# Gate products of a recurrence as 64-row passes, and a new order of ScalarE's work around them, in a hybrid transformer block

## The reference, cut to what matters

```
xb = xf.reshape(B, S, 16, 64)
r   = sigmoid(einsum('bsni,nij->bsnj', xb, w_a) + b_a)
i_g = sigmoid(einsum('bsni,nij->bsnj', xb, w_x) + b_x)
log_a = -8 * r * softplus(-lam)
a = exp(log_a)
mult = sqrt(-expm1(2 * log_a))          # 1 at the first token
h_t = a_t * h_(t-1) + mult * i_g * xf   # along the tokens
y_rnn = h * gelu(g_rnn)
```

## Time and profile before

| | |
|---|---|
| median of 3 runs | 2143.26 us (2142.67 to 2144.76) |
| the profiled execution | 2143.2 us, of it 2141.4 us span (first to last instruction) |
| TensorE busy | 2124.1 us, 99% of the span |
| TensorE weight loads | 2093.2 us, 98% |
| VectorE busy | 1684.1 us, 79% |
| ScalarE busy | 1023.3 us, 48% |
| GpSimd busy | 342.5 us, 16% |

### The profile page before, as it was taken

The page is one execution under the profiler, slowest core; times in us unless marked ns, Lnnn a source line. Parts: engine busy times, 40 slices in busy tenths (PEclk is TensorE's granted clock), DMA queues, the critical chain, the costliest instruction groups (busy, mean ns, idle before and its releaser), DMA issues.

```text
span 2141.4 us, 44252 instructions
## 1 busy us (share of the span) xinstructions
PE 2124.1 (99%) x18238; PEld 2093.2 (98%) x18238; DVE 1684.1 (79%) x2297; ACT 1023.3 (48%) x1287; POOL 342.5 (16%) x428
## 2 busy tenths in 40 slices
PE   9999999999999999999999999999999999999998
PEld 8999999999999999999999999999999999999997
DVE  7777777778855877888888888888887867767876
ACT  6555554456322554444444444444444545445543
POOL 0222222222100001212112121121211001012002
PEclk9999999999999999999999999999999999999999
DMA  5788988888543435887887878788888658679645
GB/s 178 163 195 208 209 190 204 200 186 193 155 130 99 153 112 171 233 217 212 220 217 220 225 208 221 214 224 222 230 219 277 193 155 290 177 190 278 204 138 187
DMA packets 238754, 423.84 MB, mean 198 GB/s; under 512 B 17008, under 2 KB 151792, under 8 KB 237312
## 3 DMA queue, kind: packets, MB, share of 16 engines
q1 hardware_dynamic: 147776, 256.84, 36.2%
q0 software_dynamic: 88224, 159.97, 36.0%
q10 hardware_dynamic: 2592, 4.72, 0.6%
HBM read 382.64 MB, written 89.16 MB: 220 GB/s over the span
## 4 chain that ended last, share of the span: by engine, by line
PE 93%; DVE 3%; issue 1%; ACT 1%; DMA 1%; POOL 1%; POOLq 0%; DVEq 0%; ACTq 0%
PE bank L2086 29%; PE bank L2088 29%; PE bank L2087 29%; PE bank L2470 2%; PE bank L2165 1%; PE bank L2178 1%; DVE w_all L1226 1%; DMA act_lo_f<-t_spill 1%; PE bank L2190 0%; PE bank L2189 0%; ACT act_hi L1144 0%; ACT w_all L775 0%; PE bank L2250 0%; DMA t_spill<-h_out 0%; DVE tsum L1804 0%
## 5 line engine op out<-in xcount | busy, mean ns | idle before, releaser
L2086 PE MATMUL bank<-act_hi,w_all 128*128 128x256 f32 x3272 | 909.9, 278 | 5.2 <-DVE w_all L1226 2.5
L2088 PE MATMUL bank<-act_hi,w_all 128*128 128x256 f32 x3272 | 903.9, 276 | 0.0
L2087 PE MATMUL bank<-act_lo,w_all 128*128 128x256 f32 x3272 | 903.8, 276 | 0.0
L2086 PEld LDWEIGHTS bank<-act_hi,w_all 128*128 128x128 f32 x3272 | 614.2, 188 | 11.4 <-issue 4.0
L2087 PEld LDWEIGHTS bank<-act_lo,w_all 128*128 128x128 f32 x3272 | 614.3, 188 | 0.7 <-issue 0.2
L2088 PEld LDWEIGHTS bank<-act_hi,w_all 128*128 128x128 f32 x3272 | 614.3, 188 | 0.0
L2086 PE MATMUL bank<-tsum,w_all 128*128 128x256 f32 x1280 | 353.5, 276 | 0.0
L2088 PE MATMUL bank<-tsum,w_all 128*128 128x256 f32 x1280 | 353.3, 276 | 0.0
L2087 PE MATMUL bank<-tsum,w_all 128*128 128x256 f32 x1280 | 353.3, 276 | 0.0
L1138 ACT ACTIVATE w_all<-raw_s 128x1024 fp32r<-128x1024 f32 x172 | 182.9, 1063 | 242.8 <-PE bank L2088 222.1
L1226 DVE TENSOR_TENSOR w_all<-raw,w_all 128x1024 fp32r<-128x1024 f32 x134 | 164.1, 1225 | 133.6 <-ACT w_all L775 131.9
(11 more groups left out here) (401 smaller groups left out, 3524.2 us busy)
## 6 DMA issues: line engine op xcount, KB each, us to landing
raw<-weights SPq DMA_DIRECT2D x262, 512.0 KB, 4.2
w_sums<-weights POOLq DMA_DIRECT2D x96, 512.0 KB, 6.9
raw_s<-weights SPq DMA_DIRECT2D x84, 512.0 KB, 5.4
raw_s<-weights POOLq DMA_DIRECT2D x84, 512.0 KB, 5.7
raw_a<-weights SPq DMA_DIRECT2D x66, 512.0 KB, 5.6
raw_s<-w_sums SPq DMA_DIRECT2D x48, 512.0 KB, 5.2
t_spill<-h_out POOLq DMA_DIRECT2D x48, 256.0 KB, 3.7
act_lo_f<-t_spill POOLq DMA_DIRECT2D x11, 1024.0 KB, 10.0
```

Of the source, the lines that this page charges most:

```text
L2086: pe.matmul(dst, ah, bh, start=start, stop=False, skip_group_check=goes_on)
L2087: pe.matmul(dst, ah, bl, start=False, stop=False, skip_group_check=goes_on)
L2088: return pe.matmul(dst, al, bh, start=False, stop=stop, skip_group_check=goes_on)
```

## The change

**TensorE.** The gate products become six passes of 64 rows. Pass (t, e) multiplies the 64 rows of head e with both gates' 64x64 blocks side by side, 128 columns of weights, into bank e. The passes of the two heads alternate. The block-diagonal zeros are no longer computed. Bank 0 holds gate a of head 0 over gate x of head 0; bank 1 holds gate x of head 1 over gate a of head 1.

**ScalarE.** There are four sigmoids of 64 partitions in place of two of 128. Tanh and exponential are separate now. The exponential moves behind the softmax's `exps(p * 2, 0, 4)` (in the opening behind the root). In the first pair the tanh moves ahead of the keys' high part. In the loop the split of unit u+6 moves from behind the sigmoids to ahead of the squares.

**GpSimd and VectorE.** `gw` is 128 x 2 x 64, loaded by three transfers in place of one, each time. `decay` waits for one count more, since the exponential now comes last of the three functions.

```diff
-            pool.dma_start(gw[:], gate_w[0]).then_inc(gw_landed, 16)
+            def load_gates(p):
+                pool.dma_start(gw[0:HD], gate_w[p, 0:HD, :, 0:HD]).then_inc(gw_landed, 16)
+                for g in range(2):
+                    pool.dma_start(gw[HD:P, 1 - g], gate_w[p, HD:P, g, HD:P]).then_inc(gw_landed, 16)
+            load_gates(0)
...
             def gates(p, a, b):
-                act.wait_ge(gates_done, p)
-                act.activation(rg[:], a[:], ACT.Sigmoid, bias=col("b_a", p - 1)).then_inc(gates_taken, 1)
-                act.activation(ig[:], b[:], ACT.Sigmoid, bias=col("b_x", p - 1)).then_inc(gates_taken, 1)
+                act.wait_ge(gates_done, p * 2)
+                h0, h1 = slice(0, HD), slice(HD, P)
+                for dst, bias, parts in ((rg, "b_a", ((h0, a, h0), (h1, b, h1))), (ig, "b_x", ((h0, a, h1), (h1, b, h0)))):
+                    for h, bank, at in parts:
+                        act.activation(dst[h], bank[at], ACT.Sigmoid, bias=col(bias, p - 1)[h]).then_inc(gates_taken, 1)
...
-                if first:
-                    split(u + 6, 0, MORE_MIX)
+                split(u + 6, 0, MORE_MIX)
                 attention_square(p)
                 recurrent_square(p)
-                if first:
-                    gates(p + 1, PT[0], PT[1])
-                else:
-                    gates(p + 1, PT[0], PT[1])
-                    split(u + 6, 0, MORE_MIX)
-                    gate_exponentials(p + 1)
+                gates(p + 1, PT[0], PT[1])
+                gate_tanh(p + 1)
                 high_of(k_hi, ev, k_taken, p, k_hi_done)
                 split(u + 7, 1, MORE_MIX)
-                if first:
-                    gate_exponentials(p + 1)
                 gate_root(p + 1)
                 exps(p * 2, 0, 4)
+                gate_exp(p + 1)
...
             def decay(p):
-                dve.wait_ge(gate_funcs, p * 3 - 1)
+                dve.wait_ge(gate_funcs, p * 3)
...
-                for g, bank in enumerate((a, b)):
-                    last = product(bank[:], (gw_hi[:, g], gw_lo[:, g]), (xc_hi[:], xc_lo[:]), True, True)
-                last.then_inc(gates_done, 1)
+                for t, (w, x) in enumerate(((gw_hi, xc_hi), (gw_hi, xc_lo), (gw_lo, xc_hi))):
+                    for e, bank in enumerate((a, b)):
+                        h = slice(HD * e, HD * e + HD)
+                        last = pe.matmul(bank[:], w[h].rearrange("p a n -> p (a n)"), x[h], start=t == 0, stop=t == 2)
+                        if t == 2:
+                            last.then_inc(gates_done, 1)
```

More of the change, by code:

```diff
@@ L244, in block_kernel @@
         pick = sb_in(mix, "pick", [2, P])
-        gw = sb_in(mix, "gw", [2, P])
-        gw_hi = sb_in(mix, "gw_hi", [2, P], F32R)
-        gw_lo = sb_in(mix, "gw_lo", [2, P], F32R)
+        gw = sb_in(mix, "gw", [2, HD])
+        gw_hi = sb_in(mix, "gw_hi", [2, HD], F32R)
+        gw_lo = sb_in(mix, "gw_lo", [2, HD], F32R)
+        sb_in(mix, "rest_of_gw", [6 * HD])
         stats = sb_in(mix, "stats", [3, QT])
@@ L642, in _ @@
                 pool.wait_ge(gw_split, p)
-                pool.dma_start(gw[:], gate_w[p]).then_inc(gw_landed, 16)
+                load_gates(p)
                 pool.wait_ge(s_taken, p * 6)
@@ L802, in gates, with gate_tanh, gate_root, gate_exp @@
             def gates(p, a, b):
-                act.wait_ge(gates_done, p)
-                act.activation(rg[:], a[:], ACT.Sigmoid, bias=col("b_a", p - 1)).then_inc(gates_taken, 1)
-                act.activation(ig[:], b[:], ACT.Sigmoid, bias=col("b_x", p - 1)).then_inc(gates_taken, 1)
-            def gate_exponentials(p):
-                act.wait_ge(gates_taken, p * 2)
+                act.wait_ge(gates_done, p * 2)
[3 more added lines that the diff above has]
+                        act.activation(dst[h], bank[at], ACT.Sigmoid, bias=col(bias, p - 1)[h]).then_inc(gates_taken, 1)
+            def gate_tanh(p):
+                act.wait_ge(gates_taken, p * 4)
                 act.activation(tt[:], rg[:], ACT.Tanh, scale=one_col(lam4, p - 1)).then_inc(gate_funcs, 1)
+            def gate_root(p):
+                act.wait_ge(gate_funcs, p * 3 - 2)
+                act.activation(st[:], tt[:], ACT.Sqrt).then_inc(gate_funcs, 1)
+            def gate_exp(p):
                 act.activation(ae[:], rg[:], ACT.Exp, scale=one_col(lam8, p - 1)).then_inc(gate_funcs, 1)
-            def gate_root(p):
-                act.wait_ge(gate_funcs, p * 3 - 1)
-                act.activation(st[:], tt[:], ACT.Sqrt).then_inc(gate_funcs, 1)
             def gelu(p):
@@ L822, in gate_weights @@
             def gate_weights(p):
-                act.wait_ge(gw_landed, p * 16 + 16)
+                act.wait_ge(gw_landed, p * 48 + 48)
                 act.activation(gw_hi[:], gw[:], ACT.Copy).then_inc(gw_hi_done, 1)
@@ L965, in _ @@
             act.wait_ge(negc_stored, 16)
-            gate_exponentials(1)
+            gate_tanh(1)
             gate_root(1)
+            gate_exp(1)
             pair(1, True)
@@ L2212, in pair_scores @@
                 pe.wait_ge(k_split, p + 1)
-                pe.wait_ge(gates_taken, p * 2 + 2)
+                pe.wait_ge(gates_taken, p * 4 + 4)
                 scores((0, 1))
@@ L2308, in _ @@
             pe.wait_ge(negc_ready, 1)
-            pe.wait_ge(gates_taken, 2)
+            pe.wait_ge(gates_taken, 4)
             for e, bank in enumerate((PT[0], PT[2])):
```

## The result

The changed kernel takes **2148.78 us** (median of 11 runs, 2147.53 to 2150.49), against 2143.83 us for the kernel before beside it. The ratio is 1.0024, 95% interval [1.0016, 1.0032]: slower by a quarter of a per cent. (One of the eleven executions of the kernel before took 8002.83 us; the ratio leaves it out, and the median of the other ten is 2143.70.) The forecast was 2145.2, its range ended at 2147.8; the time lies outside. The sign of the sum was right, its size was not: +5.1 us against the kernel beside it, +5.5 against the 2143.26 on which the forecast stood, where +2.0 was forecast. The profiled execution took 2148.92 us, its span is 2146.9.

The account below looks back on a forecast made before the run. TensorE was taken to bound the kernel, working through practically the whole span. Terms +1.2 - 0.3 + 1.4 + 1.5 - 1.8 = +2.0 us on 2143.26 gave 2145.2 us, 8-in-10 range 2141.2 to 2147.8.

Parts of the forecast that it names:

- The passes: Gate passes on TensorE: two 64-row passes run side by side, 1.08 us in place of 1.40, saving 0.32 us per pair.
- The opening: Kernel start: three gate loads ahead of the constants delay the warming passes and first real pass, +1.2 us; high end +1.8 more.
- The exponential ahead of the first pair: ScalarE before the first pair: exponential behind root and a second table load makes the weight split and transposes late, +1.4 us.
- The first pair: First pair's gates: four sigmoids and the tanh ahead of the keys' high part make the scores late, +1.5 us.
- The loop: Six loop pairs: load and exponential taken out pay for the added sigmoids, so 0.30 us each is saved, -1.8 us.
- if the loop's scores wait: Sign to look for in the loop: no wait at the scores expected; a wait there would show the sum wrong.
- keys' low part ends late in all six pairs: Loop rival: sigmoids at 0.69 and a split wait 0.5 later lose 0.7 us per pair, 2149.8 us; chance 0.11.
- The sum: Whole kernel: opening +1.2, its gates -0.3, exponential +1.4, first pair +1.5, loop -1.8, together +2.0 us, 2145.2 us.

Follow-up runs that it names:

- the mended kernel with 12 warming matmuls: The changed kernel with one packed gate load behind the opening's constants, exponential and tanh moved back, a one-column sigmoid loading the table early, 12 warming matmuls: 2141.46 us.

## Why the prediction was wrong, point by point

- **The passes** (0.32 us a pair, side by side): right. 0.3 measured, and 0.33 a pair where nothing else is late.
- **The opening** (+1.2): +2.3 in the trace. The loads were sized rightly (+1.13 at the first warming pass). The term mis-sized is the pace of the warming records: the working took it to quicken after as long a time as before, and its high end had all of them slow, +1.8 on top of the loads. +1.15 on top came. In other executions it was less; it belongs in the range as noise of some 0.7 us between executions of one opening. By the first scores 0.5 of it was won back, where 0.3 was reckoned.
- **The exponential ahead of the first pair** (+1.4): right, 1.3 between the first scores and the transposes. Only the place differs: TensorE waits 1.4 at a weight unit 3.6 us ahead of the transposes, and 0.6 there.
- **The first pair** (+1.5): +1.85. The order of instructions was right. From the squares to the keys' high part it is 5.94 us where 5.49 was reckoned, since all four sigmoids are 0.71 apart in place of 0.58; the squares came 0.14 earlier than reckoned and took some of that back.
- **The loop** (-1.8): +1.0 up to the last pair's scores. This step failed, and with it the sum: it makes 2.8 us of the difference, the opening with its gates 0.9, the first pair 0.35. The working had the split and the squares right to within 0.03 us, counted from the first unit pass behind the gates, and then took "a 64-row sigmoid at the same 0.58 as a 128-row one". From the first sigmoid to the tanh 2.42 us was reckoned and 2.95 came. 0.39 of these 0.53 us are the three distances of 0.71. The other 0.14 are the tanh's wait for the last sigmoid, taken at 0.1: the tanh starts 0.82 behind it, in the run with two 128-row sigmoids too. The working also left "0.2 us to spare" between the end of the keys' low part and the scores, where 0.24 passes between the two in the loop in any case. So there was no spare, and the 0.53 became scores that start 0.52 late (the list of waits books 0.46). With the passes' 0.3 won, each pair lost 0.17. The prediction had named the sign: if the loop's scores wait, the sum is wrong there.
- The working counted the loop's gain as one of the passes. The trace with the passes alone shows that they gain nothing there unless the split moves. That link was not seen; that the change moved the split as well is luck for this term.
- **The rival** "keys' low part ends late in all six pairs" was the right mechanism, with a chance of 0.11. Its condition, sigmoids at 0.69, came; its second one, a split 0.5 late, did not, and was not needed. It was given 0.7 us a pair for the two together, and 2149.8 in all. The argument against it (no load between sigmoid and tanh) said nothing on the distance of sigmoids.
- **The sum.** Forecast: 0.9, 1.4, 1.5, -1.8. Measured in the trace: 1.8, 1.3, 1.85, +1.0, and -0.4 further on in the kernel, where nothing was changed (not followed up).

## What to carry to other kernels

When a change splits an instruction by rows, look in the trace for two neighbours whose rows change as the new ones will; the distance of starts is the price, not the length that each shows. A saving on the bound engine is only as good as the spare time of the next chain: with 0.2 us left, count the time from the end of the last write to the start of the reader too, and a reader's wait for its semaphore. And before a gain is booked, look for short gaps (0.1 to 0.3 us) that no list of waits shows at the places the engine will now reach earlier.

## What the runs showed of the hardware that was not expected

- **ScalarE: change of rows.** 512-column sigmoids start 0.57 to 0.59 us apart when the second reads and writes the rows of the first, or some of them; 0.68 to 0.71 when it reads other rows, 0.70 to 0.71 when it writes other rows. The Trainium skill, ScalarE: Activation LUTs, "What ACT_TABLE_LOAD costs", has back-to-back activations overlap by about 93 ns. The traces agree for neighbours with the same rows (0.68 long, 0.59 apart) and not for the others, where the overlap is gone (0.69 long, 0.71 apart).
- **VectorE beside GpSimd's DMA issues.** Four softmax scalings per half pair take 1.27 us together in most places and up to 2.3 in some. In the run with the passes alone, first pair, VectorE and GpSimd:

```profile
153.28 2.29 DVE L1347 TENSOR_SCALAR sm<-sm,stats 128x512 f32<-128x512 f32 x4
...
153.04 1.47 POOL L631 DMA_DIRECT2D w_sums<-weights  x1 [5.68 <-DMA w_sums<-weights]
153.82 2.14 POOL L632 DMA_DIRECT2D w_sums<-weights  x1
```

  and in the kernel before, at the same place:

```profile
153.25 1.28 DVE L1346 TENSOR_SCALAR sm<-sm,stats 128x512 f32<-128x512 f32 x4
...
153.94 1.53 POOL L630 DMA_DIRECT2D w_sums<-weights  x1 [6.72 <-DMA w_sums<-weights]
```

  GpSimd began 0.9 us earlier and worked beside all four. VectorE's work behind it is 1.0 us late, and in the next pair a unit of TensorE starts 1.33 us behind the pass at 182.56 once, 1.06 of it booked as waiting for VectorE. That the two are one and the same 1.0 us is likely from their size, not shown. In the fifteen traces of sixteen such groups each, no group without an issue beside it took over 1.28. An issue beside it is not enough, though: in the run with the loads behind the constants one such group took 1.27 all the same.
- **The pace of the first passes** quickens 2.9 to 6.3 us after the first one, differently in executions of equal openings, while the granted clock reads 1.00. Behind the idle time of 3.0 us in the mended kernel with 12 warming matmuls the pace fell again (0.21 apart in place of 0.12), and there the granted clock reads 0.50. The factor is the same, so a low clock that the profile doesn't record may be behind the slow start too; no run here shows it.
- **The end of a write and the start of its reader.** A score pass that waits for VectorE's low part starts 0.24 us behind its end in the loop, and 0.10 behind it in the first pair, which stands outside the loop. Why the two differ is not shown.
